# Splitting a routing stage in two and starting row fetches inside it, in a one-core layer step

## The chip, the core and the metric

The kernel runs on one core of one Trainium2 chip. The metric is the device time of one execution in microseconds. The median of three runs of the kernel before is 3932.12 us (3922.56 to 3937.77).

## The reference, cut to what matters

One layer of a streaming encoder: 1024 prompt tokens and 64 sample tokens, width 1024. A norm and an input projection feed two mixers, whose output is added to the residual. Then comes the part that the change is about, a channel mixer of 16384 experts, each one a single neuron:

```
def block(xb):                                   # xb: tokens x 1024, normed
    qh = (xb @ peer_wq).reshape(tokens, 8, 2, 128)
    s = einsum('thpc,hpkc->thpk', qh, peer_keys)          # 2 x 128 scores for each of 8 heads
    sv, si = top_k(s, 16)
    cand = sv[:, :, 0, :, None] + sv[:, :, 1, None, :]
    cv, ci = top_k(cand.reshape(tokens, 8, 256), 16)      # 16 of the 256 sums
    eid = ...                                             # first key * 128 + second key
    gate = softmax(cv).reshape(tokens, 128)               # 128 experts for each token
    a = gelu(einsum('td,ted->te', xb, u[eid])) * gate
    return einsum('te,ted->td', a, v[eid])
```

## The kernel before, in words

All in float32. Matrix products are made from a high and a low fp32r part, as three products (high by high, high by low, low by high). The program is a row of blocks, one behind the other; at the end of a block all engines meet.

**Project and mix** (`project`, `mix`): the input projection, then both mixers and the output projection. `mix` begins by loading its constants: SP loads three (L1367 to L1369), ScalarE's queue loads four (L1380 to L1383), GpSimd's queue four columns (L1375). ScalarE then waits for all of them before its first instruction (L1386).

**Norm** (`normed_transposed`): the nine tiles of 128 tokens (the ninth has 64) are normed and transposed for the mixer. `GT = 4`: prompt tiles 0 to 3 and the 64 sample tokens, 576 in all, are "gathered" tokens; the other 512 are "dense" tokens.

**Routing** (`route`, all nine tiles at once): a loop over 8 heads, each with two key halves p. For each half SP loads a block of `wq`; ScalarE makes its high part (`high`, L431); GpSimd makes the low part (`low`, L665); TensorE makes the queries of all 1088 tokens, in chunks of 512, 512 and 64 columns with 24 products each (L486), and then the scores (L496); ScalarE copies both out of PSUM (L447, L454). VectorE finds the top 16 of both halves with five instructions for each tile (L571 to L586), forms and searches the candidate sums (L598 to L623), and writes a comparison 2304 elements wide ("stairs", L630). GpSimd multiplies it by the values (`look_up`, L672); VectorE reduces it (`first_keys_of`, L546), compares again ("hot", L555), GpSimd multiplies again, and VectorE reduces again (`second_keys_of`, L560). These steps of head h are made during head h + 1. GpSimd's own order is: the low parts of four half-heads first, and from there on, in each head, look-up 0, the two low parts of the head **two further on**, look-up 1. At the end the chosen keys and gates are turned into token columns.

**Gates** (`gate_matrices`): for each dense token a 128 x 128 matrix that holds its gates, as a product of two one-hot matrices, four tokens to a unit, 128 units. VectorE compares for one of them (L777) and, in three units of four, for the other (L780); in the fourth ScalarE does (L836, L840). GpSimd multiplies the gate in (L795), TensorE multiplies (L814), ScalarE copies out with a transpose (L843), and SP stores 4 MB for each 64 tokens (L751), eight times. The first block of `u` is loaded and split beside it (`FirstExperts`).

**Experts** (`experts`): 65 steps and a few more. In step s the dense tokens take 256 experts: 48 products for the hidden values (L1195, 512 columns each), ScalarE's gelu (L1082), VectorE's gate (L1132), the split of the result (L1039, L1136), and 48 products for the output (L1211), which VectorE adds to `y` eight times a step (L1153). The blocks of `u` and `v`, 1 MB each, are loaded and split in each step (L1088, L1141, L1074, L1122), and 0.5 MB of gates are loaded. Beside this the gathered tokens take their experts one by one: GpSimd issues an indirect DMA for each of the 576 columns of expert numbers, 128 rows of 4 KB of `u` (L1025), and as many of `v` (L1031). VectorE makes a dot product for each fetch of `u` (L1100); four fetches of `v` make a quad, for which ScalarE writes a mask (L1064) and TensorE sums (L1179). Slots for fetched rows: 6 for `u`, 10 for `v`.

The order is written out ahead by `Timetable`: fetches are numbered, u first (144 of them), from there on u and v in turn, and at last v alone; 18 to a step. The planner puts each dot, mask and quad into one of a few places in each engine's program of a step, at least ten fetches behind the fetch it needs. An engine runs its program in order, so that a late row stops all that stands behind it. The fetches themselves are issued by GpSimd in one free loop, held only by the slots.

## Time and profile before

| | |
|---|---|
| median of 3 runs | 3932.12 us |
| the profiled execution | 3930.59 us |
| its span, first to last instruction | 3928.8 us |
| mean granted TensorE clock | 0.917 |
| TensorE busy | 3275.3 us (83%) |
| VectorE busy | 2523.9 us (64%) |
| GpSimd busy | 1704.9 us (43%) |
| ScalarE busy | 1089.0 us (28%) |
| moved by DMA | 914.67 MB, 233 GB/s over the span |

In the profile PE is TensorE, DVE VectorE, ACT ScalarE, POOL GpSimd, SP the queue of the plain DMAs. A busy time is the union of an engine's instructions. Matmuls overlap, and their ends are modelled, so for TensorE the distance from one start to the next says what one costs, not its printed length; for short instructions of VectorE likewise. The stages follow one another and have different limits, so shares of the whole span say little: read them stage by stage.

### The profile page before, as it was taken

What the parts mean: (1) busy time and instruction counts of PE and PEld (TensorE: products, weight loads), DVE (VectorE), ACT (ScalarE), POOL (GpSimd) and SP (SyncE); (2) the same over time, 40 slices, a digit from 0 to 9 for tenths busy, and PEclk for the clock granted to TensorE, in tenths of its full rate; (3) what the DMA queues carried; (4) which work ended last, traced back from release to release, by engine and by line L of the source; (5) the groups of instructions that cost most, each with busy time, mean ns of one, the idle gap of its engine ahead of it and who ended that gap; (6) DMA issues with size and microseconds to landing.
All of it is one profiled execution on the core that took longest, in us unless ns stands there. A gap on an engine that the chain in (4) does not pass through costs nothing. (4 is left out here: it accounts for less than half of the span.)

```text
span 3928.8 us, 46712 instructions
## 1 busy us (share of the span) xinstructions
PE 3275.3 (83%) x17014; PEld 2498.8 (64%) x17014; DVE 2523.9 (64%) x5636; ACT 1089.0 (28%) x2099; POOL 1704.9 (43%) x1327
## 2 busy tenths in 40 slices
PE   6999478999985877296677999988999998999897
PEld 5889357778873766295455666666666665666554
DVE  3000267777742899895998777777777777776333
ACT  3111133433422111084112222222222222222221
POOL 0000000000000233295777777777777777676553
PEclk9999689999996888698888999999999999999999
DMA  3222301111113010078999999999999999999887
GB/s 134 85 91 76 123 32 47 53 36 46 37 36 114 22 32 11 3 205 263 351 352 356 411 392 392 384 407 392 391 393 379 411 388 397 383 391 363 327 337 266
DMA packets 303458, 914.67 MB, mean 233 GB/s; under 512 B 30358, under 2 KB 114478, under 8 KB 285596
## 3 DMA queue, kind: packets, MB, share of 16 engines
q0 software_dynamic: 167088, 608.95, 39.8%
q1 hardware_dynamic: 133804, 302.61, 21.8%
q8 instruction: 118, 1.93, 0.2%
q10 hardware_dynamic: 2368, 0.53, 0.1%
q14 instruction: 80, 0.66, 0.0%
HBM read 848.84 MB, written 64.32 MB: 232 GB/s over the span
## 5 line engine op out<-in xcount | busy, mean ns | idle before, releaser
L1025 POOL DMA_INDIRECT ex_row_u<-in_u_rows,eid_u x576 | 730.4, 1268 | 352.1 <-DVE ex_dots L1100 190.8
L1031 POOL DMA_INDIRECT ex_row_v<-in_v_rows,eid_v x576 | 719.0, 1248 | 289.0 <-issue 154.2
L1100 DVE CUSTOM_DVE_ANT_0 ex_row_u<-ex_row_u,ex_h2n 128x1024 f32<-128x1024 f32 x576 | 701.0, 1224 | 21.9 <-DMA ex_row_u<-in_u_rows,eid_u 21.9
L1211 PE MATMUL ex_psum_v<-ex_a_hi,ex_v_hi 128*128 128x512 f32 x1024 | 427.9, 418 | 157.0 <-DVE ex_y L1153 142.5
L1153 DVE TENSOR_TENSOR ex_y<-ex_y,ex_psum_v 128x512 f32<-128x512 f32 x504 | 339.5, 683 | 213.5 <-PE ex_psum_v L1211 180.1
L1195 PE MATMUL ex_psum_u<-h2d_hi,ex_u_hi 128*128 128x512 f32 x1024 | 411.2, 402 | 31.5 <-DMA ex_spike<-in_consts 25.3
L665 POOL TENSOR_TENSOR rt_w_lo<-rt_w_raw,rt_w_hi 128x1024 fp32r<-128x1024 f32 x16 | 37.6, 2365 | 869.7 <-ACT rt_w_hi L431 869.7
L1211 PE MATMUL ex_psum_v<-ex_a_lo,ex_v_hi 128*128 128x512 f32 x1024 | 414.8, 405 | 0.0
L1179 PE MATMUL ex_psum_g<-ex_row_v,ex_mask 128*32 128x512 f32 x2304 | 324.5, 688 | 108.3 <-ACT ex_mask L1064 89.9
L1211 PE MATMUL ex_psum_v<-ex_a_hi,ex_v_lo 128*128 128x512 f32 x1024 | 414.4, 405 | 0.0
L1195 PE MATMUL ex_psum_u<-h2d_lo,ex_u_hi 128*128 128x512 f32 x1024 | 403.2, 394 | 0.0
L1195 PE MATMUL ex_psum_u<-h2d_hi,ex_u_lo 128*128 128x512 f32 x1024 | 401.0, 392 | 0.0
L1211 PEld LDWEIGHTS ex_psum_v<-ex_a_hi,ex_v_hi 128*128 128x128 f32 x1024 | 201.3, 197 | 285.1 <-DVE ex_y L1153 158.1
L1074 ACT ACTIVATE ex_v_hi<-ex_v_raw 128x2048 fp32r<-128x2048 f32 x64 | 122.7, 1917 | 810.7 <-PE ex_psum_v L1211 673.5
L1132 DVE TENSOR_TENSOR ex_act_f<-ex_act_f,ex_gate 128x512 f32<-128x512 f32 x128 | 88.5, 691 | 357.0 <-ACT ex_act_f L1082 293.2
L1195 PEld LDWEIGHTS ex_psum_u<-h2d_hi,ex_u_hi 128*128 128x128 f32 x1024 | 193.7, 189 | 134.9 <-issue 62.8
L1179 PEld LDWEIGHTS ex_psum_g<-ex_row_v,ex_mask 128*32 128x32 f32 x2304 | 65.9, 119 | 276.9 <-issue 173.3
L1082 ACT ACTIVATE ex_act_f<-ex_psum_u 128x512 f32<-128x512 f32 x128 | 76.5, 598 | 557.5 <-PE ex_psum_u L1195 475.8
L1211 PEld LDWEIGHTS ex_psum_v<-ex_a_hi,ex_v_lo 128*128 128x128 f32 x1024 | 201.6, 197 | 45.2
L1211 PEld LDWEIGHTS ex_psum_v<-ex_a_lo,ex_v_hi 128*128 128x128 f32 x1024 | 202.2, 197 | 39.3
L1195 PEld LDWEIGHTS ex_psum_u<-h2d_hi,ex_u_lo 128*128 128x128 f32 x1024 | 193.8, 189 | 42.6
L1195 PEld LDWEIGHTS ex_psum_u<-h2d_lo,ex_u_hi 128*128 128x128 f32 x1024 | 193.8, 189 | 38.2
(298 smaller groups left out, 5700.1 us busy)
## 6 DMA issues: line engine op xcount, KB each, us to landing
ex_u_raw<-in_u SPq DMA_DIRECT2D x64, 1024.0 KB
ex_v_raw<-in_v SPq DMA_DIRECT2D x64, 1024.0 KB
gates<-gt_out SPq DMA_DIRECT2D x8, 4096.0 KB, 15.9
ex_gate<-gates SPq DMA_DIRECT2D x64, 512.0 KB
mx_pj<-proj SPq DMA_DIRECT2D x9, 1796.0 KB, 7.4
proj<-pj_out SPq DMA_DIRECT2D x63, 225.0 KB, 2.0
pj_w_raw<-in_w_in SPq DMA_DIRECT2D x6, 1800.0 KB, 7.7
ex_row_u<-in_u_rows,eid_u POOLq DMA_INDIRECT x576
```

The lines of the kernel that those rows point to most:

```text
L665: nc.gpsimd.tensor_tensor(w_lo[:, p, :, :], w_raw[:, p, :, :], w_hi[:, p, :, :].bitcast(F32), ALU.subtract).then_inc(w_low, 1)
L1025: nc.gpsimd.indirect_dma_start(row_u[:, r % UR, :], None, u_rows, bass.IndirectOffsetOnAxis(eid_u[:, r:r + 1], 0)).then_inc(u_row[r % UR], 16)
L1031: nc.gpsimd.indirect_dma_start(row_v[:, r % VR, :], None, v_rows, bass.IndirectOffsetOnAxis(eid_v[:, V_TOK[r]:V_TOK[r] + 1], 0)).then_inc( ...
L1074: nc.scalar.activation(v_hi[:, :, :], v_raw[:, :, :], ACT.Copy).then_inc(v_high, 1)
L1082: nc.scalar.activation(act_f[:, i % 2, :], psum_u[:, i % 2, :], ACT.Gelu).then_inc(active, 1)
L1100: nc.vector.tensor_tensor_reduce(row_u[:, r % UR, :], row_u[:, r % UR, :], h2n[:, n % 2, :], 1.0, 0.0, ALU.mult, ALU.add, dots[:, n % 2, r ...
L1132: nc.vector.tensor_tensor(by_block, by_block, gate[:, :, j, :], ALU.mult).then_inc(gated, 1)
L1153: ins = nc.vector.tensor_tensor(y[:, d, :], y[:, d, :], psum_v[:, i % VB, :], ALU.add)
L1179: last = nc.tensor.matmul(psum_g[VQ * q:VQ * (q + 1), half, :], mask[:, k % MR, q, :], row_v[:, (4 * k + q) % VR, half * 512:(half + 1) * ...
L1195: last = nc.tensor.matmul(psum_u[:, i % 2, :], a[:, j, k, :], b[:, k, :], start=(m == 0), stop=(m == 3 * KD - 1))
L1211: last = nc.tensor.matmul(psum_v[:, i % VB, :], a[:, j, d * P:(d + 1) * P], b[:, (s - 1) % 2, j, :], start=(m == 0), stop=(m == 3 * JG - 1))
```

## The change

- `GT = 5`: prompt tiles 0 to 4 are gathered (640 tokens), and 448 tokens are dense (tiles 5 to 7 and the sample tokens). All dense products have 448 columns in place of 512, and there are 7 blocks of gates in place of 8.
- `route` is called twice: first for the five gathered tiles, then for the dense tokens (four tiles, the last half full). With its loops written out, GpSimd's order in each head is now: look-up 0, low part of this head's second half, look-up 1, low part of the **next** head's first half.
- The second routing, the gates stage and the experts stage share one timetable and one class, `Gathered`. It has fetches at 26 to a head of the second routing, 16 to each of 14 half blocks of the gates stage, and the remaining 848 over 64 steps (13.25 each). GpSimd's fetches have places in its program too. Slots: 8 for `u` and 8 for `v`. The 1280 fetches are u alone (152), u and v in turn (976), v alone (152).
- The gates stage: VectorE makes both comparisons in all 112 units, from SBUF; the gate is multiplied in by ScalarE (four activations a unit); GpSimd only fetches. The ring is 12 deep, not 16.
- `FirstExperts` is gone: the first block of `u` is loaded and split when the experts stage begins.
- `mix`'s constants are loaded by GpSimd's queue during `project`.

The core of the diff:

```diff
-GT = 4
-DBASE = GT * P
-DTOK = SEQ - DBASE
-GTOK = TOK - DTOK
+GT = 5
+GTOK = GT * P
+DTOK = TOK - GTOK
...
         def _(pool):
...
-            def body(h, blocks_left):
-                look_up(h, 0, pick, "stairs")
-                if blocks_left:
-                    for p in range(2):
-                        low(h * 2 + 4 + p, p)
-                look_up(h, 1, look, "hot")
-            for hp in range(4):
-                low(hp, hp % 2)
...
+            low(0)
+            for h in range(PH):
+                if h:
+                    look_up(h - 1, 0, pick, "stairs")
+                meanwhile(h, 0)
+                low(2 * h + 1)
+                meanwhile(h, 1)
+                if h:
+                    look_up(h - 1, 1, look, "hot")
+                meanwhile(h, 2)
+                if h + 1 < PH:
+                    low(2 * h + 2)
+                meanwhile(h, 3)
+                meanwhile(h, 4)
...
+    OH = 12
...
+            for i in range(UNITS):
+                if i >= OH // 4:
+                    dve.wait_ge(multiplied, i + 1 - OH // 4)
+                nc.vector.tensor_tensor(hot_j[:, slot(i), :], each_key, spread(sel_j, i), ALU.is_equal)
+                nc.vector.tensor_tensor(one_i[:, slot(i), :], each_key, spread(sel_i, i),
+                                        ALU.is_equal).then_inc(compared, 1)
+                if i % 2:
+                    G.on_dve(dve, G.table.GATES + i // HALF, i % HALF // 2)
...
+            def gate(i):
+                act.wait_ge(compared, i + 1)
+                for r in range(4):
+                    at = hot_j[:, 4 * i % OH + r, :]
+                    last = nc.scalar.activation(at, at, ACT.Copy, scale=sel_g[:, 4 * i + r:4 * i + r + 1])
+                last.then_inc(gated, 1)
...
-UR, VR = 6, 10
+UR, VR = 8, 8
...
-    PER = 2 * GTOK // GROUPS
-    AHEAD = P + 16
-    DUE = 10
+    AHEAD = P + 24
+    DUE = 7
+    LANDING = 5
+    PLACES = dict(
+        route=dict(dve=(0.1, 0.25, 0.4, 0.55, 0.7, 0.85, 0.97), act=(0.3, 0.8), pe=(0.35, 0.85),
+                   pool=(0.0, 0.2, 0.4, 0.6, 0.8), sp=(0.95,)),
+        gates=dict(dve=(0.12, 0.37, 0.62, 0.87), act=(0.45, 0.95), pe=(0.5, 0.99), pool=(0.0, 0.5), sp=(0.97,)),
...
+            slot_free = dot_at.get(r - UR, 0.0) if kind == "u" else quad_at.get((r - VR) // 4, 0.0)
+            fetched = self.put("pool", self.rows, max(fetched, slot_free, self.due(f, 0)), f)
+            here = max(self.due(f, self.DUE), fetched + self.LANDING / self.rates[int(fetched)])
...
-                                    last = nc.tensor.matmul(psum_u[:, i % 2, :], a[:, j, k, :], b[:, k, :],
+                                    last = nc.tensor.matmul(psum_u[:, i % 2, 0:DTOK], a[:, j, k, :], b[:, k, :],
...
+        G = Gathered(nc, ctx, I["u_rows"], I["v_rows"], h2_tiles, x2_tile, y_rows, eid_u, eid_v, gate_n, ident_d,
+                     I["consts"][:, C_SPIKE:C_SPIKE + 2 * VQ - 1])
...
+            route(nc, "rb", hd, DTOK, I["wq"], I["keys"], ident_d, places_d, starts_d, sel=(sel_i, sel_j, sel_g),
+                  gathered=G)
```

## Rows read from the trace of the kernel before

**Rows 1.** Page, part 2: busy tenths of the DMA engines in 40 slices

```profile
DMA  3222301111113010078999999999999999999887
```

**Rows 2.** Windows: length; busy PE, PEld, DVE, ACT, POOL; granted clock, DMA share, GB/s

```profile
2155.97:3614.51 1458.54, 1320.51 (x6221) 902.01 (x6222) 1067.86 (x1509) 380.66 (x709) 1055.82 (x848) 0.95 1.00 393
3614.51:3832.95 218.44, 191.24 (x985) 117.14 (x983) 80.19 (x92) 60.62 (x149) 118.92 (x104) 0.96 0.85 326
1848.90:2155.97 307.07, 211.63 (x833) 167.85 (x833) 276.55 (x424) 57.47 (x65) 230.76 (x161) 0.85 0.94 346
1669.00:1809.00 140.00, 135.49 (x1024) 126.00 (x1024) 135.44 (x234) 126.50 (x289) 129.62 (x128) 0.97 0.77 217
...
1249.00:1669.00 420.00, 285.20 (x1467) 247.80 (x1467) 360.81 (x1948) 61.47 (x130) 118.70 (x32) 0.81 0.08 23
```

**Rows 3.** Timeline of VectorE in the routing: start us, us, engine line op

```profile
1319.74 2.55 DVE L630 TENSOR_TENSOR rt_hot<-rt_place_f,rt_starts 128x2304 f32<-128x2304 f32 x1
1322.21 1.83 DVE L571 MAX8 rt_top_v<-rt_score 128x8 f32<-128x128 f32 x9
...
1335.39 2.55 DVE L546 TENSOR_REDUCE rt_coded<-rt_hot 128x144 f32<-128x2304 f32 x1 [2.29 <-issue]
...
1367.62 2.55 DVE L630 TENSOR_TENSOR rt_hot<-rt_place_f,rt_starts 128x2304 f32<-128x2304 f32 x1
```

**Rows 4.** GpSimd's groups in the routing (count, busy us, mean ns), then TensorE's timeline there

```profile
L672 POOL TENSOR_TENSOR rt_hot<-rt_hot,rt_rise 128x2304 f32<-128x2304 f32 x8 | 40.5, 5068 | 173.4 <-DVE rt_hot L630 173.4
L665 POOL TENSOR_TENSOR rt_w_lo<-rt_w_raw,rt_w_hi 128x1024 fp32r<-128x1024 f32 x16 | 37.6, 2365 | 869.7 <-ACT rt_w_hi L431 869.7
...
1365.97 3.06 PE L496 MATMUL rt_sp<-rt_keys,rt_query 128*128 x18 [1.38 <-ACT rt_query L447]
1377.65 3.60 PE L486 MATMUL rt_qp<-h2g_hi,rt_w_hi 128*128 128x512 f32 x8 [8.62 <-POOL rt_w_lo L665]
1381.09 1.99 PE L486 MATMUL rt_qp<-h2g_lo,rt_w_hi 128*128 128x512 f32 x8
1382.92 1.30 PE L486 MATMUL rt_qp<-h2g_hi,rt_w_lo 128*128 128x512 f32 x5
```

**Rows 5.** Timeline: two dots in a row, and VectorE beside GpSimd at the routing's end

```profile
1909.36 1.23 DVE L1100 CUSTOM_DVE_ANT_0 ex_row_u<-ex_row_u,ex_h2n 128x1024 f32<-128x1024 f32 x1 [2.51 <-DMA ex_row_u<-in_u_rows,eid_u]
...
1910.51 1.22 DVE L1100 CUSTOM_DVE_ANT_0 ex_row_u<-ex_row_u,ex_h2n 128x1024 f32<-128x1024 f32 x1
...
1650.67 5.03 POOL L672 TENSOR_TENSOR rt_hot<-rt_hot,rt_top_f 128x2304 f32<-128x2304 f32 x1 [7.02 <-DVE rt_hot L555]
...
1651.21 4.65 DVE L533 TENSOR_TENSOR rt_chosen<-rt_less,rt_total 128x144 f32<-128x144 f32 x1
```

**Rows 6.** Gates stage: comparison, distance, copy out; and (page, part 6) the store

```profile
L777 DVE TENSOR_TENSOR gt_hot_j<-gt_iota_p,sel_j 128x512 f32<-128x512 f32 x128 | 84.8, 677 | 0.8 <-PE gt_psum L814 0.7
...
L836 ACT ACTIVATE gt_distance<-gt_iota,gt_minus_i 128x128 f32<-128x128 f32 x128 | 40.6, 392 | 4.5 <-DVE gt_minus_i L771 4.4
...
L843 ACT ACTIVATE gt_out<-gt_psum 128x512 f32<-128x512 f32 x128 | 68.7, 590 | 11.2 <-PE gt_psum L814 11.0
...
gates<-gt_out SPq DMA_DIRECT2D x8, 4096.0 KB, 15.9
```

**Rows 7.** GpSimd in the experts stage: one fetch, and the idle time before it

```profile
2921.35 0.94 POOL L1025 DMA_INDIRECT ex_row_u<-in_u_rows,eid_u  x1 [0.30 <-issue]
```

**Rows 8.** TensorE's timeline: products of 450 columns, a quad after a wait, a quad without

```profile
66.23 1.79 PE L334 MATMUL pj_acc<-pj_w_lo,h_hi 128*128 128x450 f32 x8
67.86 1.40 PE L334 MATMUL pj_acc<-pj_w_hi,h_hi 128*128 128x450 f32 x6
...
2807.04 3.07 PE L1179 MATMUL ex_psum_g<-ex_row_v,ex_mask 128*32 128x512 f32 x16 [2.92 <-ACT ex_mask L1064]
...
2821.64 1.92 PE L1179 MATMUL ex_psum_g<-ex_row_v,ex_mask 128*32 128x512 f32 x16
```

**Rows 9.** ScalarE's first instruction of the mix block

```profile
453.78 0.21 ACT L1386 ACTIVATE mx_dn_small<-mx_dn_small 128x4 f32<-128x4 f32 x1 [29.19 <-DMA mx_dn_small<-in_dt_bias]
```

More of the change, by code:

```diff
@@ L474, in _ @@
         def _(pe):
-            def body(h, first):
+            for h in range(PH):
                 for p in range(2):
@@ new lines, in _ @@
+            gate(0)
+            gate(1)
+            for i in range(UNITS):
+                b, q = i // Q, i % Q
+                if i + 2 < UNITS:
+                    gate(i + 2)
+                if q == 0 and b >= 2:
+                    act.wait_ge(stored[b % 2], b // 2 * 16)
+                act.wait_ge(multiplied, i + 1)
+                nc.scalar.activation(out[b % 2][:, :, 4 * q:4 * q + 4],
+                                     psum[:, i % 4, :, :].rearrange("p t j -> p j t"), ACT.Copy).then_inc(copied, 1)
+                if i % 4 == 3:
+                    G.on_act(act, G.table.GATES + i // HALF, i % HALF // 4)
@@ new lines, in __init__ @@
+        (self.dots, self.gelus, self.gates, self.turns, self.weights, self.masks, self.quads, self.adds, self.rows,
+         self.parts, self.loads) = ({} for _ in range(11))
+        dot_at, quad_at, ready, free, fetched, quad = {}, {}, {}, {-1: 0.0}, 0.0, 0.0
+        for f in fetches:
+            kind, r = f
+            n, k = r // P, r // 4
+            slot_free = dot_at.get(r - UR, 0.0) if kind == "u" else quad_at.get((r - VR) // 4, 0.0)
+            fetched = self.put("pool", self.rows, max(fetched, slot_free, self.due(f, 0)), f)
+            here = max(self.due(f, self.DUE), fetched + self.LANDING / self.rates[int(fetched)])
+            if kind == "u":
+                t = dot_at[r] = self.put("dve", self.dots, here, r)
+                if r % P == P - 1:
+                    self.put("sp", self.loads, t, n)
+                    t = self.put("act", self.gelus, t, n)
+                    t = self.put("dve", self.gates, t, n)
+                    t = self.put("pe", self.turns, t, n)
+                    ready[n] = self.put("act", self.weights, t, n) + 0.05
+            elif r % 4 == 3:
+                quad = quad_at[k] = self.put("pe", self.quads, max(here, ready[n], free[n - 1], quad), k)
+                self.put("act", self.masks, quad, k, before=True)
+                if k % QT == QT - 1:
+                    free[n] = self.put("dve", self.adds, quad, n) + 0.05
+                    self.put("sp", self.parts, free[n], n)
```

933 lines of the change are left out of this document (424 added, 509 removed).

## Prediction

> **What bounds the kernel now.** I read the windows of the stages first [rows 2], then what limits each. In the routing (1249 to 1669 us, 420 us) and the gates stage (140 us) VectorE is busy for 361 and 135 us while the DMA engines are nearly idle in the first; the slices show the same [rows 1]. In the experts stage the DMA engines are full: 47 steps take 1458.54 us, 31.0 us each, at a DMA share of 1.00 and 393 GB/s. A fetch is 128 rows of 4 KB, 0.524 MB, so 18 of them, 2.1 MB of u and v and 0.52 MB of gates are 12.06 MB, and 12.06 MB / 31.0 us is 389 GB/s. But TensorE is busy for 1320 us there too, 28.1 us a step, and idle for 2.9 us, which is one wait for ACT's mask, with a quad at a low clock behind it (3.07 us, elsewhere 1.92) [rows 2, 8]. So two resources are full at once, and taking load from one alone gives little. The first 9 steps (DVE 277 of 307 us, 18 dots each) and the last 6 (v alone, 36.4 us a step) are slower [rows 2].
>
> The change moves 432 of 1280 fetches ahead of the experts stage. I price it stage by stage, against the profiled span of 3928.8 us; that execution's own time was 3930.59 us, 0.04% below the median.
>
> **Mix.** ScalarE's first instruction comes at 453.78 after 29.19 us of waiting for constants [rows 9]. They now load during `project`. I take 27 us off, ends 20 and 29. The routing then starts at 1249 - 27 = 1222.
>
> **First routing, five tiles.** A head of nine tiles takes 1367.62 - 1319.74 = 47.9 us of VectorE [rows 3]. Twice 10.9 us of top-16 work (1322.21 to 1335.39, less the idle 2.29), four wide operations of 2.55 us and about 8 us of candidates grow with the tiles; of the remaining 8 us of short operations half is fixed. That makes 4.2 + 4.85 n: 28.5 us at five tiles, 23.6 at four. But GpSimd's new order makes a chain. From "stairs": look-up 5.07 x 5/9 = 2.8, low part 2.4 [rows 4]; 24 products of 512 columns after an idle stretch, 3.4 for the first eight (1377.65 to 1381.09) and 1.83 for each further eight, 7.1; 24 of 128 columns at some 0.11, 2.7; two copies and five scores (1.38 + 3.06 x 5/9 + 0.9), 4.0. The second half's scores are there after 19.0 us, and VectorE has only 6.1 us of work for this time. From there to the next "stairs" the second chain (first keys 4.3, look-up, low part, products, scores) takes 22.5 us, just VectorE's own 22.4. So a head takes 41.5 us, not 28.5. Before, the low parts were made two heads ahead and this was hidden. 46 us to the first "stairs", 7 x 41.5 = 290, 17 for the last look-ups and transposes: 353 us. Ends: 262 (chain hidden) and 370.
>
> **Second routing, four tiles, with fetches.** A dot costs VectorE 1910.51 - 1909.36 = 1.15 us [rows 5]. The planned rate is 26 fetches a head, u alone up to number 152; with eight slots, a landing time of 5 fetches and the given places a slot turns over three times a head, so about 24. VectorE: 23.6 + 24 x 1.15 = 51 us. DMA: 26 x 1.33 + 2.7 = 37 us; POOL: 26 x 1.24 [rows 7] and its four operations, 42 us. So VectorE bounds it, and the dots cover the chain. About 165 dots fall here: 8 x 23.6 - 8 (no key work in head 0) + 165 x 1.15, with 20 to start and 14 to end, are 405 us. To it comes one thing that the trace shows: at 1651.21 a tensor_tensor with two SBUF inputs takes 4.65 us in place of 0.31, because POOL's look-up runs (1650.67, 5.03 us) [rows 5]. A dot has two SBUF inputs too, and POOL has look-ups and low parts for 9.3 us a head. I take 2.5 us a head, 20 us; ends 0 and 8 x 9.3 = 74. Sum 425, ends 400 and 480. Both routings: 778 us in place of 420.
>
> The Trainium skill (SBUF — State Buffer, "Who interferes with whom") has this as a rule: a DVE instruction with two SBUF inputs contends with a GpSimd instruction that reads SBUF, and the later one waits in full. The trace agrees (4.65 against 0.31 us). By that rule alone an estimate of the sum would stand at its far end, 54 us later than mine.
>
> **Gates.** VectorE: 112 units x 2 comparisons x 0.60 (0.677 overlapped at the start [rows 6]) = 134, with 112 dots x 1.15 = 263 us. ACT: 4 x 0.3 + 0.5 a unit, 196 us with masks some 225 [rows 6]. POOL: 224 x 1.24 = 278. DMA: 224 fetches x 0.524 MB / 393 GB/s = 299 us, and seven stores of 4.19 MB, each 15.9 us of all engines [rows 6], which filled 0.77 of this stage before [rows 2]. If stores and fetches don't overlap, six stores add 92 us; if bytes alone count, 64. I take 376 for the body, 4 to start, 20 for the last store that nothing covers: 400 us, ends 345 and 440. DMA becomes the bound of this stage. Before it took 1669 to about 1825 (its end at 1809 and one store), 156 us.
>
> **Experts.** A 448-column product costs about 0.204 us, from eight of 450 columns in 67.86 - 66.23 = 1.63 us [rows 8]; one of 512 costs 0.229, (1382.92 - 1381.09) / 8 [rows 4]. 96 of them: 2.2 us less a step. Quads: 13.25 fetches hold 1.66 quads, not 2.25, 1.1 us less. So 28.1 - 3.3 + 2.9 idle = 27.7 us. DMA: 9.50 MB / 393 GB/s = 24.2 us, VectorE about 19: both below. The idle stays, since it is the chain gelu, gate, split on two engines; it hides under nothing. In the last 11.5 steps (v alone, 3.3 quads): 36.4 - 2.2 - 1.2 x 1.85 = 32.0. The stage before ran 24 us to the first split of u (1825 to 1848.9), 62 intervals and 96 us of end. Now 25 (u's first block loads, 1.9 + 2.3 us of splitting, on the path), 52 x 27.7 + 10 x 32.0 = 1760, and 85: 1870 us, in place of 2104. Ends: 1700 and 1930.
>
> **Sum:** 1222 + 353 + 425 + 400 + 1870 = 4270 us of span, less 5 for places I rounded up: **4265 us**, 8.5% slower. The experts stage gives 234, the mix 27; the routings take 358, the gates 244.
>
> **Rivals.** (a) **It hides better**: the low parts' chain in the first routing costs nothing (262), stores overlap the fetches (365), experts steps of 26.5 us (1795). 1222 + 262 + 410 + 365 + 1795 = 4054, with one of the three missing about 4130. For it: parts of the chain that I added up may overlap, such as the first scores and the copies. Against: TensorE did wait 8.62 us for the low part even with the old order [rows 4]. (b) **Not slower**, one mechanism: the experts steps were held by full DMA engines alone, and TensorE's idle and its cold quads were late rows. With 9.5 MB a step TensorE never waits: 96 x 0.204 + 1.66 x 1.9 = 22.7 us a step. 62 x (28.4 - 22.7) = 353 us less than 4265: 3912. It decides below 23 us a step. Against: the 2.92 us wait is for ACT's mask, not for a DMA [rows 8], and DMA alone holds a step at 24.2. (c) **Lockstep**: eight slots for each kind, POOL in program order with waits on dots and quads in front of its look-ups, dots held by POOL at the far end (+54), gates at 440, experts steps at 28.7 (+62): 4265 + 54 + 40 + 62 = 4420. For it: a dot waited 2.51 us for its row even with fetches issued in a free loop [rows 5]. (d) The fetches don't keep the timetable in the early stages and fall to the experts stage; that changes where, not how much: 4250 to 4330, inside my range.
>
> **Chances.** Forecast with (d) 0.63, (a) 0.17, (c) 0.15, (b) 0.05. The range runs from 4080, between (a) and its one-missing form, to 4410, just under (c): it leaves out (b) and about half of (a) and of (c). About 0.5%, 20 us, is what a measurement here can tell from no change. Faster takes most of (b), 0.03; the same 0.02; slower 0.95.
>
> **What would show it.** First routing: about 41 us between two "stairs", with VectorE idle for some 12 us before the second half's top-16 work, put down to ACT's score copy. Second routing: VectorE over 90% busy, 51 us a head, some dots of 2 to 5 us. Gates: DMA share 0.95 or more, dots waiting for rows. Experts: splits of u 27.7 us apart, TensorE idle 3 us a step, DMA share near 0.88. The mix starts some 27 us sooner. I am wrong if the first routing takes under 300 us, if the gates stage stays under 300, or if steps fall below 25 us.

## Result and the profile after

| | before | after |
|---|---|---|
| median, 4 runs each on one chip | 3934.94 us | 4392.42 us |
| range | 3922.56 to 3940.86 | 4390.69 to 4408.44 |
| ratio, 95% interval | | 1.1176 (1.1138 to 1.1214) |
| profiled execution: time, span | 3930.59, 3928.8 us | 4408.44, 4406.7 us |
| mean granted clock | 0.917 | 0.861 |
| TensorE, VectorE busy | 3275.3, 2523.9 us | 3212.0, 2628.3 us |
| moved by DMA | 914.67 MB, 233 GB/s | 983.49 MB, 223 GB/s |

The kernel is 11.8% slower. The direction was right and the median lies in the range, near its upper end: 127 us above the forecast. The profiled execution is the slowest of the four, 16 us above the median. The engines did no more work than before to speak of (TensorE 63 us less, VectorE 104 us more), yet the span grew by 478 us. So the time went into waits. The page's slices of the changed kernel show where TensorE stands:

```profile
PE   6999689998766623222455568888888888888887
PEclk9999699999876766666777789999999999999999
DMA  4221211111120047774899999898998998988876
```

A slice is 110 us. From the 12th to the 23rd TensorE is 20 to 70% busy and its granted clock falls to 0.6; these are the two routings and the gates stage. The windows of the stages (mix, first routing, second routing, gates, experts; columns as in [rows 2]):

```profile
440.00:1234.00 794.00, 663.59 (x4206) 538.55 (x4206) 502.88 (x1341) 292.02 (x580) 0.00 (x0) 0.89 0.17 58
1241.00:1589.00 348.00, 194.72 (x933) 165.64 (x933) 217.07 (x1175) 43.05 (x90) 83.17 (x32) 0.69 0.08 27
1589.00:2056.00 467.00, 146.31 (x589) 115.67 (x589) 406.51 (x1316) 42.89 (x79) 326.06 (x217) 0.63 0.69 231
2056.00:2546.00 490.00, 226.75 (x1377) 133.31 (x1377) 278.41 (x464) 221.35 (x683) 287.41 (x240) 0.71 0.91 321
2546.00:4406.00 1860.00, 1592.91 (x8195) 1229.39 (x8195) 1159.43 (x1611) 489.53 (x894) 1012.61 (x855) 0.95 0.88 334
```

Against my terms of the span:

| | forecast | measured |
|---|---|---|
| routing starts sooner by | 27 | 13.5 |
| first routing | 353 | 354 |
| second routing | 425 | 467 |
| gates | 400 | 490 |
| experts and end | 1870 | 1861 |

The misses add up to 13.5 + 1 + 42 + 90 - 9 = 137 us; with the 5 us that I rounded off they are the 142 us between 4265 and the profiled span, 4407. The first of them is partly chance: in the profiles of nine later runs whose kernels are the same up to there, the first routing starts at 1222.5 to 1234.8 us, and here at 1235.9.

In the first routing no engine is busy for more than 217 of 348 us. TensorE's timeline there shows it standing for the low part (`ra_w_lo`), as forecast:

```profile
1328.32 3.78 PE L485 MATMUL ra_qp<-h2g_hi,ra_w_hi 128*128 128x512 f32 x8 [2.72 <-POOL ra_w_lo L675]
...
1352.83 3.78 PE L485 MATMUL ra_qp<-h2g_hi,ra_w_hi 128*128 128x512 f32 x8 [10.71 <-POOL ra_w_lo L675]
```

The gates stage is the surprise. I had called it bound by the DMA engines, and their share is indeed 0.91. But the waits there are of another kind (what waits, for what: us in total, times, longest):

```profile
PE ga_psum L1018 <- ACT ga_mask L994: 217.2, 27, 24.4
DVE gt_hot_j L762 <- PE gt_psum L782: 150.4, 26, 9.0
ACT gt_hot_j L793 <- DVE gt_one_i L763: 140.4, 49, 20.9
POOL ga_row_v L950 <- PE ga_psum L1018: 110.6, 26, 15.1
...
DVE ga_row_u L964 <- DMA ga_row_u<-in_u_rows,eid_u: 29.8, 17, 2.8
```

TensorE waits for ScalarE, ScalarE for VectorE, VectorE for TensorE, GpSimd's fetches for TensorE's quads. Only the last of these rows is a wait for a row in flight, 30 us. That is a ring of four engines, each in its own written order. TensorE's timeline gives its beat:

```profile
2302.92 3.44 PE L1018 MATMUL ga_psum<-ga_row_v,ga_mask 128*32 128x512 f32 x16 [6.46 <-ACT ga_mask L994]
...
2317.76 2.79 PE L1018 MATMUL ga_psum<-ga_row_v,ga_mask 128*32 128x512 f32 x12 [6.46 <-ACT ga_mask L994]
```

In this stretch TensorE stands 6.46 us every four units and then runs a quad in 3.44 us, which took 1.92 in [rows 8] (the window ends inside the second quad). The stage's granted clock is 0.71; [rows 2] had 0.97 in the gates stage before.

### The profile page after: what moved, and what is told of

Same layout as the page of the kernel before. It is cut to its first block and busy times, and to the rows that moved or that the text cites. A ratio compares the mean times of both kernels' runs of the same rounds, so it can differ in the third digit from the quotient of the medians.

```text
span 4406.7 us, 46682 instructions
## 1 busy us (share of the span) xinstructions
PE 3212.0 (73%) x17132; PEld 2531.9 (57%) x17132; DVE 2628.3 (60%) x5958; ACT 1178.3 (27%) x2455; POOL 1720.8 (39%) x1366
## 2 busy tenths in 40 slices
DMA packets 314012, 983.49 MB, mean 223 GB/s; under 512 B 30183, under 2 KB 106255, under 8 KB 295997
## 5 line engine op out<-in xcount | busy, mean ns | idle before, releaser
L950 POOL DMA_INDIRECT ga_row_v<-in_v_rows,eid_v x640 | 724.1, 1131 | 882.8 <-PE ga_psum L1018 690.0
L943 POOL DMA_INDIRECT ga_row_u<-in_u_rows,eid_u x640 | 825.6, 1290 | 229.1 <-issue 185.8
L964 DVE CUSTOM_DVE_ANT_0 ga_row_u<-ga_row_u,ga_h2n 128x1024 f32<-128x1024 f32 x640 | 788.5, 1272 | 41.0 <-DMA ga_row_u<-in_u_rows,eid_u 40.7
L1018 PE MATMUL ga_psum<-ga_row_v,ga_mask 128*32 128x512 f32 x2560 | 395.0, 749 | 412.6 <-ACT ga_mask L994 337.9
L1189 PE MATMUL ex_psum_v<-ex_a_hi,ex_v_hi 128*128 128x448 f32 x1024 | 396.2, 387 | 83.5 <-DVE ex_y L1155 83.4
L1173 PE MATMUL ex_psum_u<-h2d_hi,ex_u_hi 128*128 128x448 f32 x1024 | 382.7, 374 | 23.3 <-DVE ex_u_lo L1119 23.3
L1189 PE MATMUL ex_psum_v<-ex_a_lo,ex_v_hi 128*128 128x448 f32 x1024 | 384.8, 376 | 0.0
L1189 PE MATMUL ex_psum_v<-ex_a_hi,ex_v_lo 128*128 128x448 f32 x1024 | 384.0, 375 | 0.0
L1173 PE MATMUL ex_psum_u<-h2d_hi,ex_u_lo 128*128 128x448 f32 x1024 | 376.0, 367 | 0.0
L1173 PE MATMUL ex_psum_u<-h2d_lo,ex_u_hi 128*128 128x448 f32 x1024 | 375.8, 367 | 0.0
L1189 PEld LDWEIGHTS ex_psum_v<-ex_a_lo,ex_v_hi 128*128 128x128 f32 x1024 | 199.9, 195 | 15.9
```

The costliest lines, as they stand in the source:

```text
L943: self.nc.gpsimd.indirect_dma_start(self.row_u[:, r % UR, :], None, self.u_rows, bass.IndirectOffsetOnAxis(self.eid_u[:, r:r + 1], 0)).the ...
L950: self.nc.gpsimd.indirect_dma_start(self.row_v[:, r % VR, :], None, self.v_rows, bass.IndirectOffsetOnAxis(self.eid_v[:, tok:tok + 1], 0)) ...
L964: nc.vector.tensor_tensor_reduce(row, row, self.h2n[:, n % 2, :], 1.0, 0.0, ALU.mult, ALU.add, self.dots[:, n % 2, r % P:r % P + 1]).then_ ...
L1018: last = nc.tensor.matmul(self.psum[VQ * q:VQ * (q + 1), half, :], self.mask[:, k % MR, q, :], self.row_v[:, (4 * k + q) % VR, half * 512: ...
L1173: last = nc.tensor.matmul(psum_u[:, i % 2, 0:DTOK], a[:, j, k, :], b[:, k, :], start=(m == 0), stop=(m == 3 * KD - 1))
L1189: last = nc.tensor.matmul(psum_v[:, i % VB, 0:DTOK], a[:, j, d * P:(d + 1) * P], b[:, (s - 1) % 2, j, :], start=(m == 0), stop=(m == 3 * J ...
```

## Experiments

What was on record before a run is quoted ahead of its result. "The changed kernel" has 4392.42 us; the kernel before had 3934.39, 3932.51 and 3932.23 us in the three groups of runs. The four runs of one kernel lie 4 to 42 us apart. So where there was one run alone, a difference of 20 us or less says little by itself, and I go by the stages in its profile.

### The low parts' order, first routing alone

```diff
+            if not G:
+                for hp in range(4):
+                    low(hp)
+                for h in range(PH - 1):
+                    look_up(h, 0, pick, "stairs")
+                    if h + 2 < PH:
+                        low(2 * h + 4)
+                        low(2 * h + 5)
+                    look_up(h, 1, look, "hot")
```

> The changed kernel, with GpSimd's old order in the first routing alone: four low parts first, then those of a head two heads ahead, between the two look-ups. Theory (the low parts' chain sets the pace of the first routing, 41.0 us between two stairs where VectorE has some 28 us of work): 28 to 31 us a head, the first routing ends 80 to 95 us sooner, time 4300 to 4315. Rival (TensorE's products at the low clock set the pace, and a low part in time changes little): 37 to 40 us a head, 4370 or more. The other stages keep their lengths in both.

4300.47 us (4296.05 to 4310.73), ratio 1.0934 (1.0908 to 1.0961): 92 us less. From the first "stairs" to the eighth, seven heads, in the changed kernel and then in this one (windows):

```profile
1280.50:1567.80 287.30, 162.91 (x754) 138.23 (x754) 184.23 (x1024) 32.43 (x71) 70.35 (x27) 0.68 0.06 21
```

```profile
1269.40:1461.30 191.90, 140.46 (x740) 121.07 (x738) 185.28 (x1023) 32.81 (x71) 68.87 (x26) 0.80 0.09 28
```

A head takes 27.4 us in place of 41.0, and VectorE does 184 and 185 us of work, now 97% of the stretch. The clock rises from 0.68 to 0.80, and TensorE is busy for 22 us less with the same products. The rival's 37 to 40 us a head did not come; the chain is shown as the cause.

### Masks one place earlier, gates stage

```diff
-        gates=dict(dve=(0.12, 0.37, 0.62, 0.87), act=(0.45, 0.95), pe=(0.5, 0.99), pool=(0.0, 0.5), sp=(0.97,)),
+        gates=dict(dve=(0.12, 0.37, 0.62, 0.87), act=(0.505, 0.995), pe=(0.5, 0.99), pool=(0.0, 0.5), sp=(0.97,)),
```

The timetable puts a mask at ScalarE's last place before its quad. ScalarE's place at 0.45 and TensorE's at 0.5 are the same unit of the program, so the mask came behind that unit's copy. With two numbers changed it comes four units sooner.

> The changed kernel, with ScalarE's masks in the gates stage one place (four units) earlier, so that they are made before the quad's place on TensorE comes; nothing else moves. Theory (the gates stage is a chain of four engines: TensorE stands 6.5 us at every quad for a mask that ScalarE makes only after it has copied the same unit): the stage takes 400 to 425 us in place of 470, time 4325 to 4350. Rival, my prediction (fetches and stores fill the DMA engines, and their sum sets the stage): 0 to 15 us less, time 4375 or more, with the DMA share staying near 0.91 and the dots or quads waiting for rows instead.

4321.07 us (4319.74 to 4340.23), ratio 1.0989 (1.0963 to 1.1016): 71 us less. The copies out ran from 2063.1 to 2529.3 us in the changed kernel. In this one, with the stage as a window and two waits that are not for another engine of the ring:

```profile
L805 ACT ACTIVATE gt_out<-gt_psum x112: 570/578/597, 2059.9 to 2458.4; 128x512 f32<-128x512 f32 x112
2056.00:2459.00 403.00, 228.77 (x1361) 146.23 (x1361) 278.19 (x461) 216.48 (x675) 272.31 (x239) 0.76 1.02 377
ACT gt_out L805 <- DMA gates<-gt_out: 61.6, 3, 20.6
PE ga_psum L1018 <- DMA ga_row_v<-in_v_rows,eid_v: 43.8, 16, 7.7
```

466 us became 398, and the 217 us of waiting for masks are gone. Now stores and rows do appear among the waits, at a share of 1.02 and 377 GB/s. The ring is looser and still there: TensorE waits 104.2 us for ScalarE's gate products, VectorE 79.7 us for TensorE.

### Small stores, on top of the early masks

This kernel leaves out fifteen sixteenths of every store, and the experts read the same four groups of gates again and again.

```diff
-                sp.dma_start(gates[:, :, b, :].rearrange("g i x -> i g x"),
-                             out[b % 2][:, :, :].rearrange("p (g j) t -> p g (j t)", j=JG))
+                sp.dma_start(gates[0:4, :, b, :].rearrange("g i x -> i g x"),
+                             out[b % 2][:, 0:4 * JG, :].rearrange("p (g j) t -> p g (j t)", j=JG))
...
-                                     gates[s + 1]).then_inc(gate_loaded, 16)
+                                     gates[(s + 1) % 4]).then_inc(gate_loaded, 16)
```

> The kernel with the masks of the gates stage one place earlier (4321 us), and with its seven stores cut to a sixteenth of their 4.19 MB (the experts then read those four groups of gates over and over, so the outputs of the other tiles are not the reference's). Theory (once the masks are early, the fetches and stores bind that stage, as I had predicted for the unmended one): the stage takes 310 to 350 us in place of 400, time 4250 or less. Rival (the loop of VectorE, ScalarE and TensorE still sets it): 380 us or more, the time falls by 20 to 35 us, mostly the last store and the first gates load.

4286.61 us, one run: 34 us less than with the masks alone. Copies ran from 2053.4 to 2417.1, 364 us in place of 398: between the two expectations. Behind the last copy the experts stage begins after 4 us in place of 17. So the stores cost something once the masks are early, some 34 us by the times and 47 by the two profiles. What sets the 364 us that are left is not shown: ScalarE waits 89.8 us for VectorE's comparison, TensorE 51.0 us for rows of v, and the DMA share is 0.95. My DMA term (299 for fetches and 64 to 92 for stores) named a real resource, but it was not what bound the changed kernel.

### Half rows

```diff
-                    self.row_u[:, r % UR, :], None, self.u_rows,
+                    self.row_u[:, r % UR, 0:D // 2], None, self.u_rows.rearrange("e (a d) -> (e a) d", a=2),
```

and the same for v. The kernel leaves out the second half of every gathered row; that half of the slots is cleared once.

> The changed kernel, with every gathered row cut to its first 512 numbers (2 KB in place of 4; the other half of the slots is cleared once, so the outputs of the gathered tiles are not the reference's). VectorE, TensorE and ScalarE do what they did; only the bytes of the 1280 fetches are halved. Theory (since the change TensorE's and ScalarE's order sets the gates and the experts stages, not bytes): gates stage 450 us or more (470 now), steps of the experts 26.5 us or more (27.6 now), time 4290 to 4380. Rival (bytes: the DMA engines are 0.91 busy in both stages): gates under 420 us, steps 24 to 25 us, time under 4200.

4390.3 us, one run: nothing. The same two windows (2100:2450 in the gates stage, 2600:3500 in the experts stage) of the changed kernel and of this one:

```profile
2100.00:2450.00 350.00, 168.73 (x1023) 98.69 (x1021) 207.55 (x348) 165.55 (x511) 218.89 (x183) 0.71 0.94 335
2600.00:3500.00 900.00, 784.50 (x3992) 618.12 (x3990) 624.17 (x888) 239.60 (x411) 515.48 (x432) 0.96 0.90 346
```

```profile
2100.00:2450.00 350.00, 172.88 (x1042) 100.22 (x1043) 209.80 (x351) 171.54 (x529) 220.35 (x182) 0.71 0.66 199
2600.00:3500.00 900.00, 783.62 (x3971) 615.78 (x3971) 623.99 (x889) 241.78 (x420) 532.46 (x432) 0.95 0.65 221
```

The DMA share falls from 0.94 to 0.66 and from 0.90 to 0.65, and every engine keeps its pace. The packets on the fetches' queue became fewer with the bytes (26226 and then 14630 in the first window), so it is not their number either. A DMA share of 0.9 bound nothing in the changed kernel, as it is ordered. My expectation had even allowed some gain, and there was none.

### Fetches late

One fetch to a head and one to a half block; the second edit keeps the planned landing time short at this low rate.

```diff
-IN_ROUTE, IN_GATES = 26, 16
+IN_ROUTE, IN_GATES = 1, 1
...
-            here = max(self.due(f, self.DUE), fetched + self.LANDING / self.rates[int(fetched)])
+            here = max(self.due(f, self.DUE), fetched + self.LANDING / max(self.rates[int(fetched)], 16))
```

> The changed kernel, with one fetch a head and one a half block in place of 26 and 16: nearly all 1280 fetches fall to the experts stage, 19.7 a step. What each theory expects: second routing without dots 8 heads of 34 to 38 us (its chain) in place of 57, so 320 to 340 us with its ends; gates stage 200 to 250 us, set by ScalarE (196 us of gate products and copies); experts 20 x 0.524 + 2.6 = 13.1 MB a step, 33.4 us by the DMA engines, 2200 us in place of 1850. Theory A (an early fetch costs where it stands about what it saves later): 4340 to 4430. Theory B (the early fetches alone made the kernel slower): under 4250. Theory C (early fetches pay well, as the DMA engines were the only bound of the experts stage): over 4500.

4592.62 us (4564.57 to 4606.45), ratio 1.1674 (1.1629 to 1.1719): 200 us slower than the changed kernel. The early stages did as all theories said: "stairs" of the second routing 33.9 us apart, the gates' copies in 181 us. But 62 intervals between the splits of u took 2330 us, 37.6 us each, not 33.4:

```profile
L1113 ACT ACTIVATE ex_u_hi<-ex_u_raw x63: 1892/1894/1897, 2099.1 to 4429.1; 128x2048 fp32r<-128x2048 f32 x63
2600.00:3500.00 900.00, 676.07 (x3323) 483.61 (x3320) 566.87 (x828) 195.43 (x385) 577.44 (x481) 0.86 0.92 353
PE ga_psum L1018 <- ACT ga_mask L994: 179.1, 24, 11.7
```

So theory C has the outcome and not the reason: TensorE stands 179 us of 900 for masks. The time saved early (183 us in the second routing, 285 in the gates stage) is 468 us; the experts stage took 2510 us in place of 1860, 650 more, 587 of them between these splits. The early fetches do pay, since the new experts stage is poor at carrying them: before, 18 fetches a step took 31.0 us [rows 2], here about 20 take 37.6.

### Dots with one SBUF input

```diff
+            h2 = self.h2p[:, :] if n == 0 else self.h2n[:, n % 2, :]
-            nc.vector.tensor_tensor_reduce(row, row, self.h2n[:, n % 2, :], 1.0, 0.0, ALU.mult, ALU.add,
+            nc.vector.tensor_tensor_reduce(row, row, h2, 1.0, 0.0, ALU.mult, ALU.add,
```

h2p is a PSUM tensor of 1024 columns, filled once by ScalarE. It serves the dots of the first gathered tile. In the changed kernel one of these dots stands like this beside GpSimd's low part, and two fetches like this, the first beside a dot and the second beside none:

```profile
1732.14 3.88 DVE L964 CUSTOM_DVE_ANT_0 ga_row_u<-ga_row_u,ga_h2n 128x1024 f32<-128x1024 f32 x1
1732.58 2.36 POOL L675 TENSOR_TENSOR rb_w_lo<-rb_w_raw,rb_w_hi 128x1024 fp32r<-128x1024 f32 x1
...
1704.89 1.98 POOL L943 DMA_INDIRECT ga_row_u<-in_u_rows,eid_u  x1 [0.30 <-issue]
1709.47 0.94 POOL L943 DMA_INDIRECT ga_row_u<-in_u_rows,eid_u  x1 [0.30 <-issue]
```

> The changed kernel, where the dots of the first gathered tile (128 of the 155 in the second routing, five of its eight heads) read the row from SBUF and h2 from a copy in PSUM, made once by ScalarE, so that they have one SBUF input. Theory (a dot of two SBUF inputs is held until GpSimd's look-up or low part has ended, three a head at 3.65 to 3.88 us in place of 1.2): no dot above 2 us in these heads, and a head takes 47 to 50 us in place of 55.5, time 30 to 42 us less than the changed kernel's. Rival (the long dots stand for something else, a late row or the queue): they stay, and the head stays within 2 us of 55.5.

4386.95 us, one run. Half right. Groups of dots and fetches over four heads, changed kernel (1637 to 1859) and then this one (1625 to 1843):

```profile
L964 DVE CUSTOM_DVE_ANT_0 ga_row_u<-ga_row_u,ga_h2n 128x1024 f32<-128x1024 f32 x93 | 127.6, 1433 | 0.1
L943 POOL DMA_INDIRECT ga_row_u<-in_u_rows,eid_u x95 | 135.2, 1424 | 41.4 <-issue 23.3 <-DVE ga_dots L964 17.8
```

```profile
L976 DVE CUSTOM_DVE_ANT_0 ga_row_u<-ga_row_u,rb_h2p 128x1024 f32<-128x1024 f32 x93 | 107.0, 1215 | 0.1
L952 POOL DMA_INDIRECT ga_row_u<-in_u_rows,eid_u x96 | 91.4, 952 | 49.1 <-issue 24.3 <-DVE ga_dots L976 24.2
```

All the long dots are gone (mean 1433 to 1215 ns, 5.1 us a head; there were two long ones a head, 3.65 and 3.88 us, and not three). Yet a head takes 54.8 us in place of 55.5, over the first five heads 54.6 in place of 55.6. VectorE was idle for 8.4 us in these five heads and is now idle for 21.1. Of these 15.8 stand before the reduction behind the look-up; the profile names nobody for them. That it is the chain of the low parts again, the next run shows.

### Both mended in the second routing

The last edit, the first one, and in the second routing each low part one place earlier (with `low(0)` and `low(1)` ahead of the loop):

```diff
                 meanwhile(h, 0)
-                low(2 * h + 1)
+                if h + 1 < PH:
+                    low(2 * h + 2)
                 meanwhile(h, 1)
...
-                if h + 1 < PH:
-                    low(2 * h + 2)
+                if h + 1 < PH:
+                    low(2 * h + 3)
```

> The changed kernel, with both things mended in the second routing at once: the dots of the first tile with one SBUF input, and GpSimd's low parts one place earlier (and two heads ahead in the first routing, which is worth 92 us by itself). Theory (the hold of the dots, 7.5 us a head, and the chain look-up, low part, products each hide the other, so that taking one away brought 0.7 us a head): the first heads of the second routing take 47 to 50 us in place of 55.5, time 4250 to 4275. Rival (VectorE's program is full anyway, or POOL's own time sets it): 54 us or more a head, time 4290 or more.

4286.83 us, one run: 14 us less than with the first routing mended alone, between the two expectations. The second routing is 450 us long in its profile, and 470 in that of the first routing mended alone. The first heads are 48.4 and then four times 51.9 to 52.5 us. From the first to the sixth "stairs", the changed kernel and this one:

```profile
1637.10:1914.90 277.80, 76.75 (x290) 65.64 (x290) 269.43 (x847) 22.59 (x35) 216.34 (x139) 0.61 0.74 240
```

```profile
1537.40:1794.50 257.10, 75.06 (x266) 64.30 (x266) 251.98 (x846) 22.02 (x35) 158.14 (x136) 0.61 0.71 254
```

That is 4.1 us a head for both, 1.0 over the same five heads for the hold alone. The chain alone was not taken away; since VectorE is busy for 269.4 of 277.8 us while the hold is there, I estimate at most 1.7 us a head for it. On this estimate hold and chain hid each other. What is left, 252 of 257 us, is VectorE's own work, about the 51 us a head that I had forecast; my 47 to 50 was too hopeful. The last two heads stay at 63.0 and 62.2 us.

### Masks earlier in the experts stage

```diff
-                   act=(0.08, 0.24, 0.42, 0.6),
+                   act=(0.08, 0.24, 0.45, 0.6),
```

> The changed kernel, with the second of ScalarE's four places in a step of the experts stage taken for the masks of TensorE's second place, so that they are made before the gelu of the same product and not behind it; nothing else moves. Theory (TensorE's idle time before a quad is that mask: 54.9 us in 32.6 steps, 1.7 us a step, and the quad behind it starts at a low clock): steps of 25.2 to 26.2 us in place of 27.6, time 4230 to 4310. Rival (the DMA engines, 0.91 busy, or VectorE's late sums take the wait's place): steps of 27 us or more, time 4360 or more.

4407.37 us (4403.51 to 4409.62), ratio 1.1203 (1.1184 to 1.1221), 15 us more than the changed kernel: the theory fell. Two waits of TensorE between 2600 and 3500 in the changed kernel, then what this kernel has:

```profile
PE ga_psum L1018 <- ACT ga_mask L994: 54.9, 19, 4.8
PE ex_psum_v L1189 <- DVE ex_y L1155: 52.3, 17, 5.5
```

```profile
PE ex_psum_v L1189 <- DVE ex_y L1155: 109.3, 32, 5.6
```

The wait for the mask is gone, and the wait for VectorE's sums has grown by as much, 57.0 us against 54.9. VectorE's timeline of one step of this kernel shows why: three dots before `a_lo`, then u's split and one more dot, all ahead of the first sum.

```profile
3008.50 0.62 DVE L1138 TENSOR_TENSOR ex_a_lo<-ex_act_f,ex_a_hi 128x448 fp32r<-128x448 f32 x1
3009.04 2.28 DVE L1143 TENSOR_TENSOR ex_u_lo<-ex_u_raw,ex_u_hi 128x2048 fp32r<-128x2048 f32 x1
3011.24 1.22 DVE L964 CUSTOM_DVE_ANT_0 ga_row_u<-ga_row_u,ga_h2n 128x1024 f32<-128x1024 f32 x1
3012.38 1.67 DVE L1155 TENSOR_TENSOR ex_y<-ex_y,ex_psum_v 128x448 f32<-128x448 f32 x3
```

### Dots moved too

```diff
-        dense=dict(dve=(0.1, 0.2, 0.28, 0.38, 0.46, 0.55, 0.65, 0.75, 0.85, 0.95),
+        dense=dict(dve=(0.1, 0.1, 0.38, 0.38, 0.38, 0.38, 0.6, 0.75, 0.85, 0.95),
```

Places with the time of the one before get nothing, so no dot is left between the second gate product and the first sum.

> The changed kernel with the masks of the experts stage early, as in the last run of this kind, and VectorE's dots moved out of the places between the second gate product and the first sum (they stand behind the split of v, before the second gate product and between the sums). Theory (without the mask's wait TensorE stood 3.3 us a step for the first sums, since VectorE had three or four dots and u's split in front of them): TensorE's wait for the sums falls under 1 us a step, steps of 25 to 26 us in place of 27.6, time 4240 to 4310. Rival (something else, the fetches' turnover or the splits themselves, then sets 27.6 again): steps of 27 us or more.

4282.19 us (4267.45 to 4287.05), ratio 1.0878 (1.0856 to 1.09): 110 us less than the changed kernel. The splits of u, 62 intervals, go from 2569.8 to 4195.2: 26.2 us in place of (4314.8 - 2571.4) / 62 = 28.1 over the same stretch. TensorE still waits for the sums:

```profile
PE ex_psum_v L1189 <- DVE ex_y L1155: 63.0, 35, 3.2
2600.00:3500.00 900.00, 835.55 (x4272) 660.83 (x4272) 670.23 (x955) 258.76 (x446) 602.01 (x463) 0.97 0.96 371
```

That is 1.8 us a step, not under 1. In this stage too the first wait was worth nothing until the next one was shortened with it. What the moved dots are worth without the early masks was not tried.

### The constants of the mix, in the kernel before

The class `MixConstants` and its load in `project`, as in the change, and nothing else.

> The kernel before, with one part of the change alone: the constants of the mix are loaded on GpSimd's queue during the projection. Theory: the mix starts 27 us sooner and nothing takes it back, 3900 to 3912, ratio 0.993. Rival: the loads on GpSimd's queue or the waits at the end of the projection give it back, within 5 us of the kernel before.

3917.36 us (3906.96 to 3923.56), ratio 0.9961 (0.9948 to 0.9973): 17 us, not 27. ScalarE's splits of the projection's second block of weights, in the kernel before and in this one:

```profile
70.54 3.21 ACT L302 ACTIVATE pj_w_hi<-pj_w_raw 128x3600 fp32r<-128x3600 f32 x1 [20.08 <-DMA pj_w_raw<-in_w_in]
```

```profile
87.37 3.20 ACT L306 ACTIVATE pj_w_hi<-pj_w_raw 128x3600 fp32r<-128x3600 f32 x1 [37.53 <-DMA pj_w_raw<-in_w_in]
```

The constants are issued at 62.3 us, right behind this load at 61.9, and it lands 17 us later; the projection's last copy moves from 424.0 to 434.9. The changed kernel has the same (the split at 86.98, the last copy at 433.7), which takes some 10 of the 27 us. The two medians here, 17 us apart, are the better measure of the gain than the 13.5 us between two single profiles.

```diff
         def _(pool):
+            pool.wait_ge(copied, 2 * NT)
             mc.load(pool, I)
```

> The kernel before, with the constants of the mix on GpSimd's queue as in the change, but issued only when two column blocks of the projection have been copied. Theory (issued at 62 us, the eleven loads stood in front of the second block of weights, which landed some 17 us later, and the projection ended 10 us later, so that 17 us of the 27 were left): the projection ends as before and the whole gain is there, 3903 to 3911, ratio 0.9922 to 0.9940. Rival (the weights were late for another cause, or the experts stage takes the rest back): ratio 0.9955 or more.

3919.31 us (3908.76 to 3930.78), ratio 0.9972 (0.996 to 0.9983): no better, and the rival's number. It is not the rival's reason. The second block is on time (71.98), and the fourth is late:

```profile
156.49 0.56 POOL L1370 DMA_DIRECT2D mx_consts<-in_consts  x1 [129.30 <-ACT pj_out L312]
187.54 3.20 ACT L307 ACTIVATE pj_w_hi<-pj_w_raw 128x3600 fp32r<-128x3600 f32 x1 [31.34 <-DMA pj_w_raw<-in_w_in]
```

My condition fell on the start of another load of weights, which should have been waited for 8.5 us and was waited for 31.3. The projection ended at 444.5, 20 us late. Twice the load of weights that the constants were issued beside came late, and no other. The DMA view of 61 to 90 us in the first of these kernels shows who held the DMA engines:

```profile
q0 software_dynamic: 560, 1.35, 48.8%
q1 hardware_dynamic: 1040, 1.84, 20.9%
```

The constants are q0 and the weights q1: fewer packets and fewer bytes (MB), and over twice the share of the engines' time. A start in the middle of a block, clear of both loads, was not tried.

### Everything mended

All edits above but the late fetches and those that leave something out, and a ring of 16 in place of 12 in the gates stage. The later start of the constants is among them, although it had turned out no better.

> The changed kernel with every mend at once: low parts early in both routings, masks one place early in the gates stage and the experts stage, the ring of the gates stage back at 16, dots moved in the experts stage, dots of one SBUF input, constants issued later. If each is worth what it was or should be alone, 92 + 71 + 10 + 25 + 100 us come off 4392: 4070 to 4130. If the kernel is still 3 to 5% slower than before, the loss that is left lies in the split itself: two routings of 280 and 370 us in place of one of 420, and a gates stage with dots and fetches of 390 in place of 156, against some 350 us saved in the experts stage. If it comes out under 3934, the idea was right and only its order of work was at fault.

4097.92 us (4095.86 to 4100.07), ratio 1.0421 (1.0405 to 1.0437). The stages (first routing from 1302 us on, 12.7 us behind its first "stairs"; second routing, gates, experts):

```profile
1302.00:1500.00 198.00, 120.94 (x676) 104.57 (x675) 185.89 (x993) 30.33 (x66) 66.91 (x25) 0.80 0.08 25
1500.00:1950.00 450.00, 143.76 (x589) 113.88 (x589) 385.22 (x1316) 46.06 (x89) 269.61 (x219) 0.63 0.68 242
1950.00:2368.00 418.00, 232.08 (x1377) 145.65 (x1377) 280.89 (x464) 215.55 (x675) 268.61 (x238) 0.74 1.02 375
2368.00:4097.00 1729.00, 1571.55 (x8195) 1228.05 (x8195) 1158.77 (x1611) 489.73 (x894) 1084.59 (x855) 0.96 0.93 359
```

The mends are worth 294 us, about their sum one by one (92 + 71 + 14 + 110 = 287). The deeper ring brought nothing to speak of: the gates' copies took 395 us, 398 with early masks alone. The other 166 us, 4.2% over the kernel before, are still there. The experts stage now gives 2104 - 1729 = 375 us. But the routings end at 1950 in place of 1669, and the gates stage takes 418 in place of 156: 281 + 262 = 543 us. My expectation puts what is left down to the split itself. That is not shown, since waits are left too: the last two heads of the second routing still take 62.8 and 62.0 us.

## Why the prediction was right, and where it was off

The direction rests on a mechanism that the runs bear out: the two routings and the gates stage cost more than the experts stage gives back. That the median lies in the range, 18 us inside its end, is partly luck, since the gates term had the wrong cause.

- **Mix (27 forecast, 13.5 measured between two profiles, 17 between medians in the kernel before).** I took the gain whole and looked for no cost where the loads went. The eleven loads moved past the queue of the weights and delayed one load by 17 us. I had counted what the removed wait was worth, and not what the moved transfers collide with.
- **First routing (353, measured 354).** The chain was right as a mechanism: 41.0 us between "stairs" against 41.5. Putting the order back gave 92 us, against 353 - 262 = 91. Its halves were off in opposite ways, which is luck. From the "stairs" at 1321.50 the second half's scores are copied at 1342.9, after 21.4 us (19.0 forecast), and the next "stairs" follow at 1362.66, after 19.7 (22.5 forecast; with the prices of the first chain its terms add up to 23.3). I scaled VectorE's own work from 47.9 us a head, which is the first of seven such distances; the other six are 44.7 or 44.8. With the chain gone a head took 27.1 us, not 28.5.
- **Second routing (425, measured 467).** The first five heads took 55.5 us; I had 51 and 2.5 for the held dots. VectorE's own 51 us a head was right; the run with both mended shows it. The hold was real: two dots a head of 3.65 and 3.88 us, up to 2.7 us extra each, 5.1 us a head over all dots. That is about 41 us over eight heads, where I had 20 and the far end 74. The rule of the Trainium skill (SBUF — State Buffer, "Who interferes with whom") names the right pair of instructions, and as an estimate of the size its 74 us is further off than my 20. It has the later instruction wait; in the rows above the dot begins 0.44 us before the low part and is the one that is held, as far as starts on GpSimd can be trusted. By experiment the hold is not the whole: with it gone a head got 1.0 us shorter, not 5.1. The larger miss is in the last two heads, 61.5 and 63.0 us, and some 14 us lie before the first "stairs" and behind the last (65 us in place of some 50). I gave them few dots and no cost of their own. There quads and a transpose stand in TensorE's written order ahead of the routing's products: it waits 40.4 us for the gated dots (`ga_turned`), once 21.4 us for a row of v, and VectorE 8.8 us for scores. That is the lockstep of rival (c), in two heads. With hardly any fetches there (the late fetches) all heads take 33.4 to 34.1 us, the last two among them; which of the waits makes the difference no run tells.
- **Gates (400, measured 490).** The failing step is "DMA becomes the bound of this stage". It costs the engines by their sums (VectorE 263, ScalarE 225, GpSimd 278, DMA 299 and 64 to 92) and takes the largest. The engines' sums were right: 278, 221 and 287 us are measured. (Two figures were slightly off on paper: 112 units at 1.7 us are 190 us and not 196, and six stores at 15.9 us are 95 and not 92.) None of them bound the changed kernel: the sign of a bound by DMA, dots waiting for rows, came to 30 us, and with half rows the stage's engines kept their pace. What bound it was the order in which ScalarE makes a mask, for 71 us. With that out of the way the stores cost 34 to 47 us, and what sets the rest is open. The place of the mask I could have read off the timetable's numbers and the loop: 0.45 and 0.5 are one unit. Its idle time of this kind stood in [rows 8] for the experts stage, and I did not look for it in the new one.
- **Experts (1870, measured 1861).** Steps of 27.5 us in the first 49 intervals against 27.7, 31.3 against 32.0 in the last ten, 92 against 85 at the end. I wrote that the 2.9 us of idle stay because they "hide under nothing". The size was right, the cause half: 1.7 us a step were the mask's and 1.6 the sums', and removing the first only lengthened the second. (96 products at 0.025 us less are 2.4 us, not 2.2.)
- **Rivals.** (a) is out, since its three parts all failed to come for free. (b) is out at 27.5 us a step. (c), at 4420, was nearer than my forecast to the median (28 us off, not 127), with other parts: its gates (440) were nearer than mine, its held dots (9.3 us a head, measured 5.1, mine 2.5) and its steps (28.7) were not. (d) did not happen; the fetches kept their table, and the run that forces it is 200 us slower, beyond the 4250 to 4330 I gave it.

## What to carry to other kernels

Where four engines each run a list written in advance, a stage's time need not be the largest of their sums: here it was 490 us, and the largest 287. Walk once around the ring of waits, with the places of the lists, and price that too; a mask made behind the copy of its own unit cost 71 us here, and two numbers in a table mended it. A busy share of 0.9 proves no bound: halve the load and see, as with the half rows; and ask again after each mend, since the stores did count once the masks were early. When one wait is removed and nothing moves, look for the one that took its place before giving up the theory: twice here a pair of waits was worth far more than the one that was tried alone. And a transfer that is moved lands on a queue beside others; look what is issued beside it.

## What the runs showed of the hardware that I had not expected

- **Half the bytes, the same time.** Fetches of 2 KB rows in place of 4 KB brought 4390.3 us (one run) against 4392.42, and in the gates window the DMA share fell only from 0.94 to 0.66 while the rate fell from 335 to 199 GB/s.
- **A dot lengthens GpSimd's fetch.** Issuing a fetch took 1424 ns on average in the four heads with two-input dots and 952 ns with one-input dots, over 95 and 96 of them. In the second routing of the changed kernel, fetches that overlap no dot took 0.97 us on average (83 of them), and those that overlap one 1.66 us (102), over half of them about 2.0; with one-input dots those that overlap took 0.97 us too. The hold works in both directions.
- **A few slow packets delay a large load a long way.** Two broadcast loads of 256 KB took 16.0 and 18.3 us to land, and a load of 1800 KB issued beside them came 17 and 23 us late in the two kernels (87.37 against 70.54; a wait of 31.34 where its neighbours have 8.5). The 128 packets of the broadcasts hold 4096 bytes each and took 1.5 us each in the first kernel and 1.6 in the second; the constants' packets of 6156 bytes took 0.24 and 0.34 us, the weights' of 1800 bytes 0.1. So neither size nor number makes them slow; what does, and whether they alone delay the load, no run shows.
- **A TensorE that waits pays twice.** In the seven heads of the first routing TensorE was busy with the same products for 162.9 us at a granted clock of 0.68 and for 140.5 us at 0.80; only the waits between them differed.
